# RWKV scan: block inverses by Horner's rule in the fourth power, and the key grams in the second turn

## The reference, cut to what matters

```python
def step(s, inp):
    rt, wt, kt, vt, at, bt = inp
    sa = jnp.einsum('bhij,bhj->bhi', s, at)
    s = s * wt[:, :, None, :] + sa[..., None] * bt[:, :, None, :] + vt[..., None] * kt[:, :, None, :]
    y = jnp.einsum('bhij,bhj->bhi', s, rt) if with_out else None
    return s, y
```

## Time and profile before

| | us |
|---|---|
| median of 3 runs | 3779.24 (3772.93 to 3779.87) |
| the profiled execution | 3785.26 |
| its span in the trace | 3783.5 |
| PE busy / DVE busy / ACT busy in the span | 3472.2 / 1595.7 / 1152.0 |
| mean granted TensorE clock | 0.954 |

### The profile page before, as it was taken

The page is one execution under the profiler, slowest core; times in us unless marked ns, Lnnn a source line. Parts: engine busy times, 40 slices in busy tenths (PEclk is TensorE's granted clock), DMA queues, the critical chain, the costliest instruction groups (busy, mean ns, idle before and its releaser), DMA issues.

```text
span 3783.5 us, 77347 instructions
## 1 busy us (share of the span) xinstructions
PE 3472.2 (92%) x34472; PEld 2594.7 (69%) x34472; DVE 1595.7 (42%) x3149; ACT 1152.0 (30%) x2426; POOL 387.6 (10%) x608
## 2 busy tenths in 40 slices
PE   7989998999999799799999997999999898799897
PEld 3555556788888578698888886578878676443332
DVE  1244236433333543366666664433343474311112
ACT  2233123322112323255555553222233332100001
POOL 0000013100000100122222221000010301000000
PEclk8999999999999899899999998799999899799998
DMA  5284124211111110000000001122211122489996
GB/s 196 76 338 169 45 111 179 80 55 67 67 67 62 69 45 23 7 6 5 5 5 5 5 5 72 71 89 89 108 68 45 56 92 102 175 376 428 427 428 269
DMA packets 34940, 434.13 MB, mean 115 GB/s; under 512 B 4992, under 2 KB 5600, under 8 KB 9136
## 3 DMA queue, kind: packets, MB, share of 16 engines
q1 hardware_dynamic: 29664, 413.44, 27.4%
q0 software_dynamic: 4944, 15.74, 1.3%
HBM read 423.92 MB, written 5.24 MB: 113 GB/s over the span
## 4 chain that ended last, share of the span: by engine, by line
PE 78%; DMA 9%; DVE 6%; ACT 5%; issue 1%; POOL 1%; SPq 0%; DVEq 0%; ACTq 0%; POOLq 0%
PE ps L770 16%; PE ps L1936 8%; PE ps L1938 8%; PE ps L1937 8%; PE ps L2352 7%; PE ps L3672 5%; PE ps L711 4%; DMA part<-in_wd 4%; DMA part<-in_wg 3%; PE ps L694 3%; PE ps L2345 3%; PE ps L1016 2%; PE ps L2359 2%; PE ps L2467 1%; ACT L71 1%; PE ps L2458 1%
## 5 line engine op out<-in xcount | busy, mean ns | idle before, releaser
L770 PE MATMUL ps<-part 128*128 128x512 f32 (+1 forms) x3120 | 627.1, 363 | 30.7 <-DVE part L1001 11.0
L770 PEld LDWEIGHTS ps<-part 128*128 128x128 f32 x3120 | 525.7, 194 | 132.5 <-DVE part L1001 12.2
L1936 PE MATMUL ps<-part 128*128 128x512 f32 (+1 forms) x1536 | 551.0, 359 | 18.1 <-DVE part L1983 11.4
L1937 PE MATMUL ps<-part 128*128 128x512 f32 (+1 forms) x1536 | 550.4, 358 | 0.0
L1938 PE MATMUL ps<-part 128*128 128x512 f32 (+1 forms) x1536 | 550.1, 358 | 0.0
L3672 PE MATMUL ps<-part 128*64 128x512 f32 x1536 | 375.7, 612 | 37.2 <-DMA part<-in_wd 15.9
L1960 DVE TENSOR_TENSOR part<-part 128x1024 fp32r<-128x1024 f32 x128 | 158.2, 1236 | 499.8 <-ACT part L1949 499.8
L2352 PE MATMUL ps<-part 64*64 64x64 f32 x9984 | 343.7, 220 | 20.7 <-ACT part L2675 11.9
L2352 PEld LDWEIGHTS ps<-part 64*64 64x64 f32 x9984 | 318.2, 136 | 48.8 <-ACT part L2675 12.8
L1936 PEld LDWEIGHTS ps<-part 128*128 128x128 f32 x1536 | 290.1, 189 | 68.1 <-DVE part L1983 12.6
L1937 PEld LDWEIGHTS ps<-part 128*128 128x128 f32 x1536 | 291.6, 190 | 46.5
(11 more groups left out here) (405 smaller groups left out, 4677.8 us busy)
## 6 DMA issues: line engine op xcount, KB each, us to landing
part<-in_ada_w SPq DMA_DIRECT2D x36, 2048.0 KB, 8.8
part<-in_mlp_w SPq DMA_DIRECT2D x32, 2048.0 KB, 7.6
part<-in_wg SPq DMA_DIRECT2D x32, 2048.0 KB, 22.2
part<-in_wu SPq DMA_DIRECT2D x32, 2048.0 KB, 22.5
part<-in_wd SPq DMA_DIRECT2D x32, 2048.0 KB, 22.2
part<-in_b_in SPq DMA_DIRECT2D x8, 2048.0 KB, 7.8
part<-in_ab_w_in SPq DMA_DIRECT2D x7, 2048.0 KB, 7.5
part<-in_rkv SPq DMA_DIRECT2D x6, 2048.0 KB, 7.4
```

The lines of the kernel that those rows point to most:

```text
L770: mm = pe.e.matmul(ps[:, j * n:j * n + n], lhs, rhs, start=k == ks[0] and i == 0, stop=k == ks[-1] and i == 2)
L1936: pe.e.matmul(ps, wh[:, k, :], hi[:, k, x0:x1], start=k == 0, stop=False)
L1937: pe.e.matmul(ps, wh[:, k, :], lo[:, k, x0:x1], start=False, stop=False)
```

## The change

The fourth power is the last one made. The sum of the 16 powers is (I + Q(I + Q(I + Q)))·X1, where Q is the fourth power and X1 the sum of the powers 0 to 3; it is taken by Horner's rule in turns 4, 5 and 6, in a new tile Y. The second squaring is one product in place of two, the third is gone. There is one product with X and one addition more. The steps after it (X transposed, PX, XM) move one turn back each, from turns 6 to 9 to turns 7 to 10. The key grams "ka" and their masking move from turn 10 to turn 1.

```diff
-        s.NP, s.M, s.Pf = K.alloc(2, 4, 64), K.alloc(4, 64), K.alloc(4, 64)
+        s.NP, s.Y, s.M, s.Pf = K.alloc(2, 4, 64), K.alloc(4, 64), K.alloc(4, 64), K.alloc(4, 64)
@@ rw_pe
-            if turn == 10:
+            if turn == 1:
                 ps = K.bank("ka", *u.key).rearrange("p (g x c) -> p g x c", g=4, x=2)
                 gram(u, ps[:, :, 0:2 if u.lat else 1, :], u.ks, u.ops[:, to, :]).then_inc(*pe.up(("ka", *u.key)))
...
-            if turn in (3, 4, 5):
+            if turn in (3, 4, 5, 6):
                 lev = turn - 3
                 ps = K.bank(("X add", lev), *u.key)
-                pe.wait_ge(K.at("NP", *u.key, lev + 1), K.at("X", *u.key, lev))
-                blocks(ps, 0, NP[:, 1, :, :], XX[:, 0, :, :]).then_inc(*pe.up((("X add", lev), *u.key)))
-            if turn in (2, 3, 4):
+                pe.wait_ge(K.at("NP", *u.key, min(lev + 1, 2)), K.at("X", *u.key, lev))
+                blocks(ps, 0, NP[:, 1, :, :], s.Y if lev > 1 else XX[:, 0, :, :]).then_inc(
+                    *pe.up((("X add", lev), *u.key)))
+            if turn in (2, 3):
                 lev = turn - 2
                 ps = K.bank(("squares", lev), *u.key)
                 pe.wait_ge(K.at("NP", *u.key, lev))
-                if lev < 2:
+                if lev == 0:
                     blocks(ps, 0, NP[:, 1, :, :], NP[:, 0, :, :])
                 blocks(ps, 256, NP[:, 0, :, :], NP[:, 1, :, :]).then_inc(*pe.up((("squares", lev), *u.key)))
-            if turn == 6:
+            if turn == 7:
                 ps = K.bank("X turned", *u.key)
...
-            if turn in (6, 8):
-                lev = turn // 2 - 2
+                lev = (turn - 5) // 2
                 ps = K.bank(("PX", lev), *u.key)
...
-            if turn in (7, 9):
-                lev = (turn - 5) // 2
+            if turn in (8, 10):
+                lev = turn // 2 - 3
                 ps = K.bank(("XM", lev), *u.key)
@@ rw_dve
-            if turn == 10:
                 w = 128 if u.lat else 64
                 v.wait_ge(K.at("ka", *u.key))
...
-            if turn in (3, 4, 5):
+            if turn in (3, 4, 5, 6):
                 lev = turn - 3
                 v.wait_ge(v.now(), K.at(("X add", lev), *u.key))
-                v.e.tensor_tensor(XX[:, 0, :, :], XX[:, 0, :, :],
+                v.e.tensor_tensor(s.Y if lev in (1, 2) else XX[:, 0, :, :], XX[:, 0, :, :],
...
-            if turn in (6, 8):
-                lev = turn // 2 - 2
+            if turn in (7, 9):
+                lev = (turn - 5) // 2
                 v.wait_ge(v.now(), K.at(("PX", lev), *u.key))
...
-            if turn in (7, 9):
-                lev = (turn - 5) // 2
+            if turn in (8, 10):
+                lev = turn // 2 - 3
                 v.wait_ge(v.now(), K.at(("XM", lev), *u.key))
@@ rw_act
-            if turn in (2, 3, 4):
+            if turn in (2, 3):
                 lev = turn - 2
-                o = 0 if lev < 2 else 256
+                o = 256 * lev
                 s.wait_ge(K.at(("squares", lev), *u.key), K.at("X", *u.key, 0))
...
-            if turn == 6:
+            if turn == 7:
                 s.wait_ge(K.at("X turned", *u.key))
```

More of the change, by code:

```diff
@@ L2407, in rw_pe @@
                 pe.wait_ge(K.at("NP", *u.key, lev))
-                if lev < 2:
+                if lev == 0:
                     blocks(ps, 0, NP[:, 1, :, :], NP[:, 0, :, :])
                 blocks(ps, 256, NP[:, 0, :, :], NP[:, 1, :, :]).then_inc(*pe.up((("squares", lev), *u.key)))
-            if turn == 6:
+            if turn == 7:
                 ps = K.bank("X turned", *u.key)
-                pe.wait_ge(K.at("X", *u.key, 3))
+                pe.wait_ge(K.at("X", *u.key, 4))
                 turned(ps, 0, [XX[:, 0, g, :] for g in range(4)]).then_inc(*pe.up(("X turned", *u.key)))
-            if turn in (6, 8):
-                lev = turn // 2 - 2
-                ps = K.bank(("PX", lev), *u.key)
-                pe.wait_ge(K.at("X", *u.key, lev + 2), K.at("Pf", *u.key))
-                blocks(ps, 0, Pf, XX[:, 0, :, :]).then_inc(*pe.up((("PX", lev), *u.key)))
             if turn in (7, 9):
                 lev = (turn - 5) // 2
+                ps = K.bank(("PX", lev), *u.key)
+                pe.wait_ge(K.at("X", *u.key, lev + 3), K.at("Pf", *u.key))
+                blocks(ps, 0, Pf, XX[:, 0, :, :]).then_inc(*pe.up((("PX", lev), *u.key)))
+            if turn in (8, 10):
+                lev = turn // 2 - 3
                 ps = K.bank(("XM", lev), *u.key)
@@ L2446, in rw_pe @@
                 ps = K.bank("uu", *c)
-                pe.wait_ge(K.at("rh in", *c), K.at("X", *u.key, 5))
+                pe.wait_ge(K.at("rh in", *c), K.at("X", *u.key, 6))
                 for hd, o in halves():
@@ L2559, in rw_dve @@
                 if u.n:
-                    v.wait_ge(K.at(("X add", 2), u.d, u.n - 1))
+                    v.wait_ge(K.at(("X add", 3), u.d, u.n - 1))
                 v.wait_ge(K.at("gram", *u.key))
@@ L2603, in rw_dve @@
                 v.e.tensor_tensor(w, w, K.ps.of(("XM", lev), *u.key)[:, 0:512 if lev == 1 else 256], ADD).then_inc(
-                    *v.up(("X", *u.key, lev + 3), free(("XM", lev), *u.key)))
+                    *v.up(("X", *u.key, lev + 4), free(("XM", lev), *u.key)))
         if what == "stream" and turn % 3 == 2:
```

## The result

The changed kernel takes 3827.27 us (median of 4, 3820.98 to 3829.62) against 3776.09 (median of 4). The ratio is 1.0132 with a 95% interval of 1.0119 to 1.0144: 51 us slower. I had forecast 3777.6 and no change, with a range up to 3792, so the prediction was wrong.

The account below looks back on a forecast made before the run. The stage looked bound by TensorE, but in turns 4 to 6 by VectorE. Plain rounds +3.4, round 0 +1.3, round 23 -1.5 and heavy rounds -4.8 summed to -1.6 us: about 3777.6, range 3763 to 3792.

Parts of the forecast that it names:

- TensorE is relieved in turns 3 to 6 and VectorE takes the gain back: Plain round: TensorE's work alone would give -0.93 us, but VectorE's 5.26 us series makes it +0.24.
- the one on the key grams: Move of ka from turn 10 to turn 1: claimed to cost TensorE nothing, with room for VectorE's two masks of 0.69.
- the 0.33 us ahead of uu in turn 1: TensorE's wait in turn 1 of a plain round, claimed to go because ka stands before uu: -0.33 us.
- In turn 10 TensorE loses a filler, but turn 11 needs nothing of the solve: Turn 10 after ka moves away: no loss expected there, beyond 0.09 us allowed for XM waiting for M.
- Horner's rule, with -1.6: Whole forecast sum: plain rounds +3.4, round 0 +1.3, round 23 -1.5, heavy rounds -4.8 us, together -1.6.
- +0.24 each: Plain rounds: 28.95 us forecast against 28.71, over fourteen rounds +3.4 us.
- half of a clock step: Heavy rounds: half of a possible 1.5 us gain taken in five rounds, -3.8, with -0.5 each for rounds 1 and 22.
- My two slower ones: Clock falls in plain rounds, 3800 us, chance 0.09; or a longer VectorE series, 3792 or so, chance 0.09.
- the fourth: Rival: both extra additions and the turn 10 wait lie bare, +0.84 plain, +1 heavy, 3792 or so; chance 0.09.
- the wait in turn 10: XM waiting for M with only rh between; 0.09 us allowed in the forecast, lying bare in a slower rival.
- The clock did not fall in plain rounds: Rival judged: clock takes turns 4 to 6 for rest, 1.56 us a plain round, +22, 3800 us; chance 0.09.
- TensorE bounds the stage after all: Rival: VectorE's series gets out of the way, -31 us, 3748, or 3763 with half of it; chance 0.10.

## Why the prediction was wrong

**What held.** TensorE is relieved in turns 3 to 6 and VectorE takes the gain back: X transposed was to start 8.86 us after turn 3, and it started at 2162.93 - 2154.05 = 8.88. The waits on the addition are there. In the heavy round y var was to come 12.0 after turn 3 and the end 28.4; they came at 12.09 and 28.61. The round was longer than forecast all the same, 40.31 us for 38.6, since ahead of turn 3 it took 11.70 and not 10.2. These rows are the timeline of PEld in that round of the changed kernel:

```profile
2115.69 0.54 PEld L2352 LDWEIGHTS ps<-part 64*64 64x64 f32 x16 [0.76 <-ACT part L2724]
...
2127.78 0.30 PEld L2480 LDWEIGHTS ps<-part 128*128 128x128 f32 x2
...
2135.09 1.04 PEld L2352 LDWEIGHTS ps<-part 64*64 64x64 f32 x32 [1.27 <-DVE part L2603]
...
2144.30 1.95 PEld L2345 LDWEIGHTS ps<-part 64*64 64x64 f32 x64
```

XM of direction 1 came 7.31 after y var, with 7.3 forecast. The row names VectorE, but L2603 had only direction 0's work; ScalarE's copy for direction 1 (L2728) ran from 2134.61 to 2134.97, just ahead of the start at 2135.09, and putting that copy on VectorE took the wait away.

**The step that failed** is the one on the key grams: "The move costs TensorE nothing in itself: the same instructions, earlier." The instructions were the same, their neighbours were not. I counted instructions by a mean duration and did not ask what ran beside them. The trace of before has the lora products of both directions next to each other, and the weight loads of L2376 as x4 in 0.31 us where one by itself is 0.19 long (its median); the change puts the key grams between them. It cost 26 to 30 us. The same step let the key grams cover the 0.33 us ahead of uu in turn 1; the gap is part of the lora products' own 1.07 us and stayed, 8 us over 24 rounds (this I read from the rows, no run takes it away). And "In turn 10 TensorE loses a filler, but turn 11 needs nothing of the solve" looked at the wrong turn: what waits is in turn 10 itself, uu without Horner's rule (0.42 us a round, above) and with it XM, which waits for M. I allowed 0.09 for that; a round of the changed kernel with a context unit shows 0.69 (the matmul row names L2596, which makes M, with 0.58):

```profile
2099.50 0.54 PEld L2352 LDWEIGHTS ps<-part 64*64 64x64 f32 x16
2100.73 0.57 PEld L2352 LDWEIGHTS ps<-part 64*64 64x64 f32 x16 [0.69 <-issue]
```

**A term that was mis-sized** is Horner's rule, with -1.6 in a sum that took the covered gap of turn 1 as won. Alone it measured +12 (8 to 16). The +0.39 and +0.55 of plain rounds make 6.6 us in fourteen, where I had +0.24 each. The heavy rounds, where I had taken back half of a clock step, got longer instead, by some 7 us in six: in rows of 2 us each the granted clock is at 0.5 for about 3.4 us in three of them and for about 6.8 in the other three, where the kernel before has 3.4 in five and none in the sixth. Round 0 took 25.48 for 23.64 (31.61 in the changed kernel, mostly by the clock, as the last section shows). These are rows of one execution each, so they need not add up to 12.

**The rivals.** My two slower ones had the right sign by the wrong mechanism; of the fourth only the wait in turn 10 came. The clock did not fall in plain rounds: in rows of 2 us each it is down only in rounds 0, 4, 7, 13, 19 and 22 of the changed kernel. That TensorE bounds the stage after all is refuted by the experiment with early preparing steps: only with VectorE's work moved away did Horner's rule pay.

The Trainium skill would have warned me. "TensorEngine Tiling (Array Packing)", section "Key Properties", says that different tiles can load weights and multiply in parallel, and that a change of tiling mode drains TensorE. The trace agrees with the first: 1.07 us for the pair against 1.05 for one. The gap of 0.33 us behind the 64*128 products, whatever 64*64 product follows, is what the second would leave; no run tells it from another cause.

## What to carry to other kernels

Before moving matmuls, look at what stands next to them on TensorE: products on different rows of the array that are neighbours in the order can cost as much together as one, and here key grams or uu put between them made each pay in full. An engine whose work is cut gains only down to the next series of the engine beside it; here the gain was VectorE's to give, and moving two of its steps one turn turned +12 us into -10. Where one engine's order is changed, see which copy ends up behind a long block and whether another engine can make it; that was worth some 8 us here.

## What the runs showed of the hardware

A matmul pair of 64x128 weights on rows 0 to 63 and 64 to 127 took 1.07 us side by side (the kernel before and the one with the key grams behind the pair) and 1.05 to 1.06 each apart (the changed kernel and the one with the pair parted alone). Going back from 64*128 to 64*64 products TensorE's weight loads stood still for 0.33 us in all of them. Going to 64*128 they did for 0.17 us behind the key grams, and for only 0.07 behind uu (2129.84 to 2129.91) and rh. The profile names the gap of 0.33 now by "issue", now by a ScalarE copy that had ended just then, so a releaser there is no proof of a wait.

Round 0 took 31.61 us in the changed kernel and 23.64 in the kernel before, and most of that is the granted clock. The scan begins at 0.50, 1.2 GHz, in both; the kernel before leaves it after 4.0 us (1583.1 to 1587.1), the changed one after some 13 (1574.4 to 1587.4), though TensorE is busy all the time. Columns as in the earlier trace rows; the second row is a fall later in the round, in its turns 6 to 8:

```profile
1576.00:1586.00 10.00, 10.00 (x120) 8.09 (x118) 2.81 (x6) 2.54 (x7) 0.00 (x0) 0.50 0.01 2
```

```profile
1595.00:1600.00 5.00, 5.00 (x136) 4.88 (x134) 3.21 (x8) 1.99 (x6) 3.66 (x6) 0.76 0.01 3
```

By my estimate the 9 us more at half the clock cost 4.5 us. The fall came behind three waits of 0.84, 0.84 and 0.51 us; with about 3.4 us at 0.5 (rows from 1594 to 1598) it cost 1.7. The kernel with the key grams behind the pair left the low clock after some 4 us, so whether the long start belongs to the change or to this execution stays open.

The heavy rounds of one kernel have several lengths, and the clock's rows go with them: in the kernel before five of these rounds take 40.12 to 40.17 us, with the granted clock at 0.5 for about 3.4 us, and the sixth takes 38.59 with 1.00 throughout. In the changed kernel they take 40.31 and 40.35 us without a fall, 41.12 and 41.31 with one, 41.86 and 42.07 with two.
